# RWKV output projection: steps between the scan products of pass 16, kept z fetched in four groups, another order of tiles

## The reference

```python
    y = _wkv7_scan(r, decay, k, v, -kk, kk * a.astype(jnp.float32))
    mean = jnp.mean(y, axis=-1, keepdims=True)
    var = jnp.mean(jnp.square(y - mean), axis=-1, keepdims=True)
    y = ((y - mean) * lax.rsqrt(var + GN_EPS)).reshape(B, L, D_INNER)
    y = y * ln_w.astype(jnp.float32) + ln_b.astype(jnp.float32)
    bonus = (jnp.sum(r * k * r_k, axis=-1, keepdims=True) * v).reshape(B, L, D_INNER)
    y = (y + bonus.astype(jnp.float32)).astype(x.dtype) * jax.nn.silu(g)
    return y @ w_out
```

## Time and profile before

| what | value |
|---|---|
| time, median of 3 runs | 2368.23 us (2368.07 to 2373.46) |
| profiled execution: time, span | 2372.47 us, 2370.7 us |
| PE busy | 2300.3 us, 97% of the span |
| DVE, ACT, POOL busy | 1221.8, 851.0, 1141.2 us |
| pass 16 and 17 on PE, by the timeline | 1668 to 1770 us |
| the projection's remaining units | 1770 to 1839 us |

### The profile page before, as it was taken

How to read it: one execution, slowest core, us unless ns; L and a number is a source line. 1 busy time by engine, 2 the same in 40 slices (tenths; PEclk the granted TensorE clock), 3 DMA queues, 4 the chain that set the end, 5 groups by cost and what they waited for, 6 DMA issues and landing times.

```text
span 2370.7 us, 51852 instructions
## 1 busy us (share of the span) xinstructions
PE 2300.3 (97%) x22065; PEld 1793.3 (76%) x22065; DVE 1221.8 (52%) x2284; ACT 851.0 (36%) x1762; POOL 1141.2 (48%) x771
## 2 busy tenths in 40 slices
PE   8999999999999999999999999999899999999998
PEld 7788887788887677777777777777689787877776
DVE  4353278577803655555555555555430475555521
ACT  4122112233302355555555555555320343433300
POOL 4555566866663433334443444333446353343345
PEclk9999999999999999999999999999799999999999
DMA  3332332233322212222222222221513331221212
GB/s 111 82 80 80 81 97 83 86 98 98 107 97 66 92 57 66 66 66 71 70 66 66 66 66 68 73 66 56 183 55 116 106 81 41 61 61 41 94 58 94
DMA packets 263757, 188.07 MB, mean 79 GB/s; under 512 B 18267, under 2 KB 242393, under 8 KB 263145
## 3 DMA queue, kind: packets, MB, share of 16 engines
q1 hardware_dynamic: 263529, 184.76, 26.0%
HBM read 162.69 MB, written 22.04 MB: 78 GB/s over the span
## 4 chain that ended last, share of the span: by engine, by line
PE 59%; DVE 3%; POOL 1%; DMA 1%; issue 1%; ACT 0%; SPq 0%; POOLq 0%; DVEq 0%
PE ps L1348 18%; PE ps L159 7%; PE ps L160 6%; PE ps L161 6%; PE ps L1510 3%; PE ps L1526 3%; PE ps L1552 2%; PE ps L1499 2%; PE ps L2388 2%; PE ps L1466 2%; PE ps L1438 1%; PE ps L1361 1%; PE ps L221 1%; DMA z_lo<-z_kept 1%; PE ps L2374 1%; PE ps L1483 1%
## 5 line engine op out<-in xcount | busy, mean ns | idle before, releaser
L150 POOL TENSOR_TENSOR w_lo<-raw,w_hi 128x1024 fp32r<-128x1024 f32 (+1 forms) x196 | 494.7, 2524 | 16.4
L147 POOL TENSOR_SCALAR w_hi<-raw 128x1024 fp32r<-128x1024 f32 (+1 forms) x196 | 215.9, 1101 | 562.2 <-PE ps L161 544.7
L159 PE MATMUL ps<-h_hi,w_hi 128*128 128x512 f32 x616 | 244.4, 397 | 4.8 <-POOL w_lo L150 4.6
L161 PE MATMUL ps<-h_hi,w_lo 128*128 128x512 f32 x616 | 240.7, 391 | 0.0
L160 PE MATMUL ps<-h_lo,w_hi 128*128 128x512 f32 x616 | 240.7, 391 | 0.0
L1885 POOL TENSOR_TENSOR kp<-k_b,kp 128x528 f32<-128x528 f32 x16 | 29.5, 1846 | 364.7 <-ACT kp L1647 364.7
L1348 PE MATMUL ps<-mixed_r,raw 128*64 128x264 f32 x1024 | 155.1, 393 | 2.3 <-ACT g_b L1589 2.3
L159 PEld LDWEIGHTS ps<-h_hi,w_hi 128*128 128x128 f32 x616 | 116.2, 189 | 30.7 <-POOL w_lo L150 7.2
L1348 PE MATMUL ps<-mixed_k,raw 128*64 128x264 f32 x1024 | 138.4, 390 | 0.0
L161 PEld LDWEIGHTS ps<-h_hi,w_lo 128*128 128x128 f32 x616 | 116.1, 188 | 24.9
L160 PEld LDWEIGHTS ps<-h_lo,w_hi 128*128 128x128 f32 x616 | 116.2, 189 | 23.0
(11 more groups left out here) (447 smaller groups left out, 5856.4 us busy)
## 6 DMA issues: line engine op xcount, KB each, us to landing
raw<-in_rwkv_w_in_dram SPq DMA_DIRECT2D x64, 512.0 KB, 4.1
raw<-in_w_up_dram SPq DMA_DIRECT2D x44, 512.0 KB, 3.8
raw<-in_w_in_dram SPq DMA_DIRECT2D x41, 512.0 KB, 3.8
raw<-in_w_down_dram SPq DMA_DIRECT2D x22, 512.0 KB, 3.5
raw<-in_mla_w_in_dram SPq DMA_DIRECT2D x22, 512.0 KB, 4.0
sb_kept<-xT SPq DMA_DIRECT2D x16, 528.0 KB, 3.0
xT<-sb_kept SPq DMA_DIRECT2D x16, 528.0 KB, 4.4
raw<-in_rwkv_w_out_dram SPq DMA_DIRECT2D x16, 512.0 KB, 4.5
```

Source lines behind the costliest of these rows:

```text
L147: nc.gpsimd.tensor_scalar(w_hi[s][:, 0:width], raw[s][:, 0:width], 1.0, 0.0, ALU.mult, ALU.add).then_inc(split_hi, 1)
L150: nc.gpsimd.tensor_tensor(w_lo[s][:, 0:width], raw[s][:, 0:width], w_hi[s][:, 0:width].bitcast(F32), ALU.subtract).then_inc(split_ready, 1)
L159: nc.tensor.matmul(dst, w[0], x[0], start=start, stop=False)
L161: return nc.tensor.matmul(dst, w[1], x[0], start=False, stop=stop)
```

## The change

- The steps of the projection begin in the scan of pass 16: units 0 to 3 are PE's filling of pass 16 (one step in each of the three places of a link, one behind the scan, none in the turn), units 4 to 7 that of pass 17 (2, 1 and 2 steps in a link).
- POOL splits unit 0 within pass 15, between the bk products and the sb products, and unit 1 at the end of part A of pass 15; units 2 and 3 in pass 16, 4 to 8 in pass 17.
- z_hi and z_lo become one buffer z_both, so that one transfer brings both parts of a pair. The kept z comes in four groups of 3, 4, 4 and 2 pairs, each with its own semaphore; the first is issued in pass 15 when a_mm, which counts the items of part A, is at 188 of 192, the others at 190, at 192 and at the start of pass 16's body on SP. PE waits for a group at its first pair.
- The tiles come in another order (7 before 5 and 6), with other banks and other waits, and ACT's partial_out(0) moves to just behind the turn of pass 16, partial_out(1) to pass 16's end.
- The slots are now taken by n % 2 in place of (U_WO + n) % 2. U_WO is odd, so unit 17 and the first unit of mla_in meet in one slot, and that one's split and load wait for it.

```diff
-        WO_TILES = [(0, 0), (0, 1), (1, 0), (1, 1), (2, 0), (2, 1), (3, 0), (4, 0), (3, 1), (4, 1), (5, 0), (5, 1), (6, 0), (6, 1),
-                    "left_a", "left_b", (7, 0), (7, 1)]
-        WO_BANKS = [(0, 1), (0, 1), (4, 7), (2, 3), (0, 1), (2, 3), (0, 1), (4, 5)]
+        WO_TILES = [(0, 0), (0, 1), (1, 0), (1, 1), (2, 0), (2, 1), (3, 0), (4, 0), (7, 0), (3, 1), (4, 1), (7, 1), (5, 0), (5, 1),
+                    "left_a", "left_b", (6, 0), (6, 1)]
+        WO_BANKS = [(0, 1), (0, 1), (4, 7), (0, 1), (2, 3), (0, 1), (4, 5), (4, 5)]
...
-                        pe.wait_ge(s_z, 48)
...
+                for g, (first, _) in enumerate(Z_LOADS):
+                    if n < 2 and k == first:
+                        pe.wait_ge(z_here[g], 16)
...
-            if i > PAIRS:
-                steps = itertools.chain.from_iterable(wo_unit(pe, n) for n in range(2, 7))
+            if i >= PAIRS:
+                steps = itertools.chain.from_iterable(wo_unit(pe, n) for n in (range(4) if i == PAIRS else range(4, 8)))
+            per_link = FILL_S if A else (1, 1, 1) if i == PAIRS else (2, 1, 2)
...
             if i == PAIRS:
-                steps = itertools.chain.from_iterable(wo_unit(pe, n) for n in range(2))
+                fill(1)
...
-                fill(FILL_TURN)
+                if A:
+                    fill(FILL_TURN)
...
+                if i == PAIRS - 1:
+                    wo_split(pool, 0)
                 pool.wait_ge(gs_ev, 2 * i + 2)
...
-            for n in {PAIRS: (0, 1, 2), PAIRS + 1: (3, 4, 5, 6, 7, 8)}.get(i, ()):
-                split_unit(pool, U_WO + n, (U_WO + n) % 2)
+            for n in {PAIRS - 1: (1,), PAIRS: (2, 3), PAIRS + 1: (4, 5, 6, 7, 8)}.get(i, ()):
+                wo_split(pool, n)
...
+        def first_loads(sp):
+
+            sp.wait_ge(a_mm, 12 * PAIRS - 4)
+            sp.wait_ge(s_zk, 16 * READY)
+            load_z(sp, 0)
+            sp.wait_ge(a_mm, 12 * PAIRS - 2)
+            wo_load(sp, 0)
+            load_z(sp, 1)
             sp.wait_ge(a_mm, 12 * PAIRS)
...
+            wo_load(sp, 1)
+            load_z(sp, 2)
...
+                pool.wait_ge(unit_done, U_IN)
                 for u in range(U_IN, UNIT_AT["B", 0] + 1):
```

More of the change, by code:

```diff
@@ L1266, in program @@
         z_kept = nc.dram_tensor("z_kept", [PAIRS, P, 2, T2], F32, kind="Internal").ap()
-        s_wa, s_sbk, s_sbl, s_zk, s_z = (sem(n) for n in ("s_wa", "s_sbk", "s_sbl", "s_zk", "s_z"))
+        s_wa, s_sbk, s_sbl, s_zk = (sem(n) for n in ("s_wa", "s_sbk", "s_sbl", "s_zk"))
+        Z_LOADS = [(0, 3), (3, 7), (7, 11), (11, 13)]
+        z_here = [sem(f"z_here{q}") for q in range(len(Z_LOADS))]
         pads = sem("pads")
@@ L1407, in wo_unit @@
                     x = z_hi[:, k, at:at + T2 // 2], z_lo[:, k, at:at + T2 // 2]
-                    mm = product(ps[:, banks[h], 0:T2 // 2], block_of(u % 2, b), x, start, stop)
+                    mm = product(ps[:, banks[h], 0:T2 // 2], block_of(n % 2, b), x, start, stop)
                     if h == 1 and q == len(todo) - 1:
@@ L1458, in pass_pe @@
                     mm.then_inc(u_mm, 1)
-                fill(FILL_S[1] if A else 2)
+                fill(per_link[1])
                 if Cs:
@@ L1712, in pass_act @@
                 turned()
+            if i == PAIRS:
+                partial_out(0)
             if A:
@@ L1741, in pass_act @@
             if i == PAIRS:
-                partial_out(0)
+                partial_out(1)
             if A:
@@ L1878, in pass_dve, with wo_split @@
                 nc.vector.tensor_tensor(yn_b, y_c[:, PAD:TP], ysq_b, ALU.mult).then_inc(yn_ev, 1)
+        def wo_split(pool, n):
+            u, s = U_WO + n, n % 2
+            pool.wait_ge(landed[s], landings(u + 1 - 2 * s, s))
+            pool.wait_ge(unit_done, U_WO if n == 0 else u - 1)
+            pool.sem_inc(unit_taken, 1)
+            nc.gpsimd.tensor_scalar(w_hi[s][:, 0:1024], raw[s][:, 0:1024], 1.0, 0.0, ALU.mult, ALU.add).then_inc(split_hi, 1)
+            pool.wait_ge(split_hi, u + 1)
+            nc.gpsimd.tensor_tensor(w_lo[s][:, 0:1024], raw[s][:, 0:1024], w_hi[s][:, 0:1024].bitcast(F32),
+                                    ALU.subtract).then_inc(split_ready, 1)
+            pool.wait_ge(split_ready, u + 1)
         def pass_pool(pool, i, A, B, Cs):
@@ L1959, in wo_load, with load_z, last_loads @@
                 src = out_src(rw_out, P * m, half)
[L1960 to L1965, removed]
-            sp.wait_ge(a_mm, 12 * PAIRS)
[L1968 to L1972, removed]
+            sp.wait_ge(split_ready, U_WO if n == 0 else u - 1)
+            _, k, cols = src.shape
+            sp.dma_start(raw[n % 2][:, 0:k * cols].rearrange("p (k n) -> p k n", k=k), src).then_inc(landed[n % 2], 16)
+        def load_z(sp, q):
+            p0, p1 = Z_LOADS[q]
+            sp.dma_start(z_both[:, p0:p1, :, :].rearrange("p a b n -> p a (b n)").bitcast(F32),
+                         z_kept[p0:p1, :, :, :].rearrange("a p b n -> p a (b n)")).then_inc(z_here[q], 16)
+        def first_loads(sp):
[5 more added lines that the diff above has]
+            load_z(sp, 1)
+            sp.wait_ge(a_mm, 12 * PAIRS)
+            wo_load(sp, 1)
+            load_z(sp, 2)
+        def last_loads(sp):
             for done, n in ((a_ev, 12), (fa, 14), (pa, 13), (scanned, 1)):
                 sp.wait_ge(done, n * PAIRS)
-            load_z(sp, z_lo, 1, 6, READY)
+            load_z(sp, 3)
         def pass_sp(sp, i, A, B, Cs):
@@ L1988, in pass_sp @@
             if i == PAIRS:
-                wo_load(sp, 2)
+                for n in (2, 3):
+                    wo_load(sp, n)
             if A:
@@ L2000, in pass_sp @@
                 next_weights(1, 8, 3, i)
+                if last:
+                    first_loads(sp)
                 if not last:
@@ L2558, in _ @@
                     pass_sp(sp, i, i < PAIRS, 1 <= i <= PAIRS, i >= 2)
-                for n in range(5, 11):
+                for n in range(6, 11):
                     wo_load(sp, n)
@@ L2626, in _ @@
                 all_passes(pe, pass_pe)
-                sums_after = {10: (0,), 11: (1,), 13: (2,), 14: (3,), 15: (4, 5), 16: (6,), 17: (7,)}
-                for n in range(7, 18):
+                sums_after = {11: (0,), 12: (1,), 13: (2,), 14: (3,), 15: (4, 5), 16: (6,), 17: (7,)}
+                for n in range(8, 18):
                     for _ in wo_unit(pe, n):
```

33 lines of the change are left out of this document (21 added, 12 removed).

## The result

| | median us | lowest to highest | executions |
|---|---|---|---|
| before | 2369.24 | 2368.07 to 2373.46 | 4 |
| changed | 2394.91 | 2394.80 to 2395.82 | 4 |

The ratio is 1.0104, 95% interval 1.0092 to 1.0116: slower by 25.7 us. The forecast was 2376.8 (2370 to 2382), so the direction was right and the size a third of what came.

A forecast was written before the change was run, and what follows sets the result against it. TensorE, busy 97%, bounds the kernel where it idles or runs at half clock. Terms 0.7 + 1.4 + 10.4 - 3.2 + 2.0 - 4.7 + 2.0 = +8.6 us gave 2376.8 us, range 2370 to 2382.

The forecast's parts named there:

- z and weights: Before pass 16's first projection step: the 3.89 us wait for kept z goes, hidden behind the scan with some 11 us spare.
- The wait for unit 0: Link 0 of pass 16's scan: PE waits 5.7 us for POOL's split, ready at 1674.45.
- The filled scan: Pass 16's scan with one step in each place: 25.3 us at full clock, plus 2.0 for half clock.
- The clock term: Pass 16's filled scan: half clock lasts 4.4 to 6.2 us, costing 1.8 to 3.1; 2.0 us taken.
- The rivals: Four other outcomes: cheap clock (0.33), clock falling again at the turn (0.04), faster (0.06), z late all the same (0.02).
- three signs of being wrong: Pass 17's wait under 5 us, clock at 1.00 through the waits, or pass 16's filled scan taking 21 us.
- The turn: Behind pass 16's scan: Gram begins 3.1 us after the turn, ACT's copy being the later one.
- Rival 2: Clock falls once more at pass 16's turn, Gram 3.7 instead of 2.2 us: +2 to +4, 2379 to 2381; chance 0.04.
- The wait for unit 4: Link 0 of pass 17: PE waits over 10 us for a split behind POOL's z steps; 10.4 in the sum.
- Rival 3: Faster: pass 17's first unit is ready without the 10.4 us, later clock terms go too, down to 2359; chance 0.06.
- Pass 17's scan and unit 9: Scan of 31.4 us plus 2.0 for clock, then a 3.5 us wait for unit 9's split instead of 1.1.
- The tail: Start of mla_in: its first split, ready 3.7 us behind the last step, costs nothing, with 5 us of cover.

The follow-up runs named there:

- e7: The kernel before with only the z fetch changed (one buffer z_both, four groups, a wait per group): 2361.68 us, 0.9971 of before.
- e2: The changed kernel with unit 0's split moved ahead of POOL's wait for rn in pass 15: 2375.88 us, 1.0025 of before.
- e1: The changed kernel with thirteen unread products on PE just ahead of its wait for unit 0's split: 2379.81 us, 1.0043 of before.
- e3: The changed kernel with pass 16's steps put closer: five per link in links 0 to 4, two in link 5: 2386.08 us, 1.0067 of before.
- e8: The changed kernel with unit 0 split before POOL's rn wait, unit 3 kept for pass 17 and unit 4 split earlier: 2358.81 us, 0.9963 of before.
- e5: The changed kernel with unit 3 kept for pass 17, unit 4 split before z of pair 14, partial_out(1) moved into pass 17's scan: 2386.73 us, 1.0069.
- e4: The changed kernel with POOL's split of mla_in's second unit held until DVE's first sum is done: 2400.85 us, 1.0126 of before.

## Why the prediction was right in direction and wrong in size

**z and weights: right.** The idle time ended by a DMA is gone, worth 7 us by itself (e7), of which 3.9 are the wait and the rest the half clock behind it.

**The wait for unit 0: right.** 5.7 forecast, 5.89 measured; e2 shows that POOL's order makes it.

**The filled scan: the step that failed.** The prediction says "After work was dense again it stayed at half for 6.2 us in one case (1699.8 to 1706) and 4.4 in the other", and takes 2.0 us. Its full-clock part, 25.3 us, was right within 0.2 us (e1: 25.5, e2: 25.4). The clock term was 2.0 and measured 16.7 (42.2 - 25.5). In both rows that it came from, PE did other work than in the links: four steps on end and then Gram in the first, the transposes and first products of mla_in in the second. In a link one step of three products stands between groups of 4 to 12 small ones (64 columns). That the clock would come back among these as it did there was assumed and had no row. Worse, held a warning: in the bare scan before, the same small products left the clock at 0.50 for 19.8 us with PE busy 14.2. The bounds should have run from 1.8 us to the case that it doesn't come back at all: at the prediction's own 0.6 of the pace the 25.3 us become 42.2, 16.9 more, and the time 2376.8 + 14.9 = 2391.7. The rivals didn't have this case either: all of them took the return of the clock for certain and asked only how soon. None of the prediction's three signs of being wrong looked for it: they ask for a short wait, a clock that stays up and a scan of 21 us, and the scan took twice that. e3 bears the cause out from the other side: with five steps to a link the clock came back after 7 us.

A rule could have misled in the same way. The Trainium skill ("TensorE: Matmul & The Clock Gate", Part 1) says that full clock comes back after a short stretch of sustained matmul work. The rows at 1755.7 and 1804.4 agree (3 and 5 us); the row at 1669.9 does not, if what the profile shows as busy is taken for sustained work (42 us), and the measurement decides.

**The turn: half right.** ACT's copy is the later one, as said (0.49 us idle, ended by bk_rows), but Gram came 4.1 instead of 3.1 us after the turn's start, because the turn still ran at half clock: at full clock it is 3.2 us (e8: 1689.85 to 1693.01). Gram itself and all up to pass 17 took 29.18 us for 29.1. Rival 2 didn't happen as put: the clock didn't fall at the turn, it rose in it (1714.7, in the nine transposes). In e1, e2 and e8 it stays at 1.00 through a turn without steps.

**The wait for unit 4: right.** 10.7 forecast from row to row, 10.32 measured, and e5 takes it away by order alone. Rival 3 didn't happen, since the unit was not ready.

**Pass 17's scan and unit 9: right.** 49.3 forecast, 48.71 measured, with a wait of 3.34 us for 3.5, and the clock term behind the wait, 2.0, measured 2.8 (55.79 - 52.97).

**The tail: wrong by 2.6 us.** The prediction says "Nothing, with 5 us of cover". The split was covered as it says, but it now runs beside DVE's first two instructions behind the last norm. The sum took 2.73 us for 0.71 beside w_lo, and the instruction ahead of it 1.34 for 0.77 beside w_hi (POOL's from 1862.66 to 1863.70): 2.6 us together, which is the whole growth of PE's wait (5.75 for 3.16). Cover was thought of as time alone, not as who else works then. Two rows of the kernel before show both without a split beside them (DVE timeline):

```profile
1843.06 0.77 DVE L2750 SCALAR_TENSOR_TENSOR mT<-mT,params,norm_r 128x528 f32<-128x528 f32 x1 [3.39 <-ACT norm_r L215]
1843.86 0.71 DVE L2753 TENSOR_TENSOR xT<-xT,mT 128x528 f32<-128x528 f32 x1
```

What is left open: why one step in each place leaves the clock down and five steps to a link bring it back. The runs show the two cases, not the measure by which they differ. The new slots, the order of the tiles and the moved partial_out were not run apart either; only the slots' cost at the tail is read from rows. And the steps in the scan bring less than it seems: e8 and e7 reach pass 17 nearly at the same time (55.8 and 56.5 us), e8 with 16 more steps done by then, 5.8 us of work. Of this, 2.6 us go at the tail and 1.2 at unit 9 (a wait of 2.26 us for 1.03), and with the 0.7 us from the start 2.7 are left.

## What to carry to other kernels

Where a change puts a wait on PE in front of a chain of small products, count the wait, and as a bound of the range the whole chain at half clock; then look for idle time of the releasing engine further up: here moving one split out of the way was worth 19 us, more than the wait of 5.9. When steps are moved to an earlier place, walk down the order of the engine that prepares their inputs and see which unit is asked for first afterwards; one unit kept back took away a wait of 10 us. And run the parts of such a change alone: here the fetch of z alone was a gain of 7 us, hidden by the rest.

## What the runs showed of the hardware

- PE showed as busy for 42.26 of 42.30 us, and its clock stayed at 1.2 GHz all the time (changed kernel, 1669.9 to 1712.2; 42.23 us for the same stretch in e4 and e5). With thirteen unread products in the wait (e1) the same stretch ran at 2.4 GHz.
- A DVE instruction with two inputs from the on-chip memory took 2.73 and 2.85 us beside POOL's w_lo, which has two as well, and 0.71 and 0.76 alone; w_lo took 2.67 and 2.68 for 2.34. In both pairs DVE began later and ended about 0.6 us behind POOL (1867.0 and 1866.5; 1873.9 and 1873.3), nearly its whole length alone. Beside w_hi, which has one such input, DVE was slower too: 1.34 for 0.77 (changed kernel) and 1.42 for 0.71 (e4). The Trainium skill ("GPSIMD Engine Reference", Specifications) says that the two engines share their memory interfaces, with contention when a VectorE instruction has two such inputs: the rows agree, and show it beside w_hi as well.
